# A fused decoder step on one core: the fourth group's output projection placed behind the second group's queries, with one planner table shifted by eight rows

## What is computed

```python
proj = hn @ w_in                      # hn = normed, modulated x
...                                   # retention and RG-LRU, gated and summed: merged
x = x + g1 * (merged @ w_out)         # the output projection
hn2 = rmsnorm(x, norm2_w) * (1.0 + sc2) + sh2
q = (hn2 @ w_q).reshape(T, 8, 256)    # 8 heads, two halves of 128
s1, s2 = q[..., :128] @ k1.T, q[..., 128:] @ k2.T       # 128 keys each
# top 16 of each, top 16 of their 256 sums: 8 * 16 = 128 experts a token
act = gelu(einsum('td,tkd->tk', hn2, u_tab[expert]))    # 128 rows of peer_u a token
x = x + g2 * einsum('tk,tkd->td', g * act, v_tab[expert])
y = rmsnorm(x, final_norm_w)
```

## Time and profile before

| | us |
|---|---|
| median of 3 runs | 3495.47 (3483.97 to 3502.88) |
| the profiled execution | 3501.91 |
| its span, first to last instruction | 3499.9 |
| TensorE busy | 3207.5 |
| VectorE busy | 2702.7 |
| GpSimd busy | 1826.4 |
| ScalarE busy | 1384.4 |

### The profile page before, as it was taken

One profiled execution on the slowest core, in us unless ns is written; L12 is line 12 of the kernel. 1 busy time (PEld: TensorE's weight loads), 2 busy tenths in 40 slices (PEclk: granted clock), 3 DMA queues, 4 the chain that ended last, 5 costly groups with the idle time before them and its releaser, 6 DMA issues.

```text
span 3499.9 us, 57521 instructions
## 1 busy us (share of the span) xinstructions
PE 3207.5 (92%) x18226; PEld 2582.7 (74%) x18226; DVE 2702.7 (77%) x5874; ACT 1384.4 (40%) x3092; POOL 1826.4 (52%) x1436
## 2 busy tenths in 40 slices
PE   6999998999999989887999999999998999998665
PEld 4777766666666668776878888888887888877555
DVE  3333357998998887889899999999998887667665
ACT  4444311333333221487555555555654565000110
POOL 0000002555567663345666766666665675766775
PEclk9999999999999999999999999999999999999888
DMA  8444454788899998789999999999999999999998
GB/s 269 150 150 150 140 173 150 258 273 283 264 336 331 317 331 305 270 281 361 380 392 391 403 389 393 388 391 397 398 356 374 388 406 407 396 410 407 372 353 301
DMA packets 429467, 1127.33 MB, mean 322 GB/s; under 512 B 42112, under 2 KB 166400, under 8 KB 429312
## 3 DMA queue, kind: packets, MB, share of 16 engines
q0 software_dynamic: 204800, 745.10, 57.0%
q1 hardware_dynamic: 219744, 370.53, 29.7%
q10 hardware_dynamic: 4768, 9.96, 0.8%
HBM read 1098.83 MB, written 26.62 MB: 322 GB/s over the span
## 4 chain that ended last, share of the span: by engine, by line
PE 38%; DVE 19%; DMA 13%; issue 12%; POOL 4%; ACT 1%; another core or an unknown queue 0%; POOLq 0%; DVEq 0%; ACTq 0%; SPq 0%
PE vacc L2355 21%; DVE rows L1754 8%; DMA rows<-in_peer_u,eidx 8%; PE scat L2289 5%; PE vacc L934 4%; POOL rows L1567 3%; DMA vbuf<-in_peer_v 2%; PE vacc L2269 2%; PE scat L2342 2%; PE vacc L905 1%; DVE oh1w L1835 1%; DVE hot L1650 1%; POOL W L1567 1%; DMA rows<-in_peer_v,eidx 1%; DMA rows<-in_peer_v,dots 1%
## 5 line engine op out<-in xcount | busy, mean ns | idle before, releaser
L1567 POOL DMA_INDIRECT rows<-in_peer_u,eidx x1080 | 1421.8, 1317 | 1456.3 <-DVE dots L1754 587.2
L2355 PE MATMUL vacc<-W,vbuf 128*128 (+1 forms) x6144 | 1426.7, 388 | 34.8 <-DMA vbuf<-in_peer_v 28.7
L1754 DVE CUSTOM_DVE_ANT_0 rows<-rows,htok 128x1024 f32<-128x1024 f32 x1080 | 1289.2, 1218 | 148.0 <-DMA rows<-in_peer_u,eidx 132.1
L2355 PEld LDWEIGHTS vacc<-W,vbuf 128*128 128x128 f32 x6144 | 1158.0, 193 | 185.6 <-issue 35.7
L2089 ACT ACTIVATE oh<-iota,e2s 128x128 bf16<-128x128 f32 x1536 | 486.4, 390 | 16.0 <-DMA scratch_sc<-sqb 7.0
L934 PE MATMUL vacc<-W 128*128 128x384 f32 x1280 | 431.6, 494 | 1.2 <-ACTq L811 1.2
L934 PEld LDWEIGHTS vacc<-W 128*128 128x128 f32 x1280 | 242.0, 192 | 169.1 <-issue 7.5
L2096 ACT ACTIVATE W<-scat 128x256 f32 (+1 forms) x320 | 122.9, 384 | 555.0 <-PE scat L2342 520.9
L2092 ACT ACTIVATE oh<-oh,ones 128x512 bf16<-128x512 bf16 x384 | 277.3, 722 | 12.5
L1835 DVE TENSOR_TENSOR oh1w<-oh,wpart 128x768 bf16<-128x768 bf16 x384 | 213.8, 557 | 62.6 <-PE scat L2342 43.1
L2289 PE MATMUL scat<-W 128*128 128x256 f32 (+1 forms) x1024 | 248.5, 398 | 5.4 <-DVE W L1636 5.4
(11 more groups left out here) (345 smaller groups left out, 3184.4 us busy)
## 6 DMA issues: line engine op xcount, KB each, us to landing
vbuf<-in_peer_v SPq DMA_DIRECT2D x384, 512.0 KB
W<-in_w_in SPq DMA_DIRECT2D x80, 512.0 KB
W<-in_wq SPq DMA_DIRECT2D x64, 512.0 KB
vbuf<-in_w_ada SPq DMA_DIRECT2D x9, 2048.0 KB, 8.0
rows<-in_peer_u,eidx POOLq DMA_INDIRECT x1080
W<-in_w_in SPq DMA_DIRECT2D x16, 1024.0 KB
W<-in_w_ada SPq DMA_DIRECT2D x3, 2048.0 KB, 15.8
W<-in_w_out SPq DMA_DIRECT2D x12, 512.0 KB, 10.0
```

Source lines behind the costliest of these rows:

```text
L1567: g.indirect_dma_start(row_of[s], None, table[:, :], bass.IndirectOffsetOnAxis(ap=picked, axis=0)).then_inc(landed[s], 16)
L1754: v.tensor_tensor_reduce(row_of[s], row_of[s], htok[:, home, :], 1.0, 0.0, ALU.mult, ALU.add, dots_of(t)[:, c:c + 1]).then_inc(used, 1)
L2355: mm = pe.matmul(vacc[:, k, :], vbuf[:, s, k * P:(k + 1) * P], W[:, e1, :].rearrange("p o t -> p (o t)"), start=(clear and s == 0 and k % ...
```

## The change

On TensorE `mixed(3)` moves behind `cross(1)`. `turn(0)` and `sum_squares(1)` move into `mixed(2)`, behind its chunks 1 and 3, and `turn(1)` behind it, ahead of `cross(1)`, with a wait until VectorE has finished `picks_high(1)`. On VectorE `residual(2)` takes `picks_high(0)`, `picks_low(1)` (behind chunk 1) and `scale(1)` (behind chunk 3) inside, `picks_high(1)` follows it, and `residual(3)` comes last, ahead of quarter -2, with ten jobs and eight pieces. Part B's last three `fill()` calls get no jobs. The table gives 341 jobs instead of 350 to part B's end, 400 instead of 388 to the start of quarter -2, and eight more at every cut from quarter 0 on. The projection's weight loads get two semaphores, so that its first part waits for the first two loads alone; the store of group 3's x goes behind eight more query weight loads on SyncE's queue; ScalarE's squares of group 3 go from inside `cross(1)` to behind it.

```diff
-AHEAD = 20
+AHEAD = 28
-HALF_B, END_B = 160, 350
+HALF_B, CALM_B, END_B, CALM = 160, 304, 341, 3
...
-            ("n", HALF_B, END_B, 12, 12, SLOTS * H // 2), ("z", END_B, q, 12, 12, 2 * KC),
-            ("r", q, q, 12, 14, 16), ("s", q, q + 4, 14, 15, 8)]
-    cuts = [q + 4, q + 36, q + 76] + [q + P + AHEAD + 64 * i for i in range(10)]
-    units = [15, 17, 19.5, 21.5, 23.5, 25.5, 27.625, 29.625, 31.75, 33.875, 36, 36, 36]
+            ("n", HALF_B, CALM_B, 12, 12, SLOTS * (H // 2 - 1)), ("o", CALM_B, END_B, 12, 12, SLOTS - CALM), ("z", END_B, q, 12, 12, KC + 4),
+            ("r", q, q, 12, 14, 16), ("s", q, q + 6, 14, 15, 8),
+            ("t", q + 6, q + 16, 15, 15.5, KC)]
+    cuts = [q + 16, q + 48, q + 84] + [q + P + AHEAD + 64 * i for i in range(10)]
+    units = [15.5, 17.5, 19.75, 21.75, 23.75, 25.75, 28, 29.75, 31.75, 33.875, 36, 36, 36]
...
             if k0 == 0:
-                pe.wait_ge(wo_in, 96 * g + 96)
+                pe.wait_ge(wo_low, 32 * g + 32)
...
+                pe.wait_ge(wo_in, 64 * g + 64)
...
-                slots = steps(plan[4])
-                residual(2, lambda: mixed_step(next(slots)))
-                picks_high(0)
-                scale(1)
-                residual(3, lambda: mixed_step(next(slots)))
+                slots = steps(plan[5])
+                residual(2, lambda: mixed_step(next(slots)), {1: first_turned, 3: lambda: scale(1)})
+                picks_high(1)
+                for at in slots:
+                    mixed_step(at)
...
+                slots = steps(plan[8])
+                residual(3, lambda: mixed_step(next(slots)))
+                for row in plan[9:]:
...
-                mixed(2)
-                turn(0)
-                sum_squares(1)
-                mixed(3)
-                cross(1, later)
+                mixed(2, {2: lambda: turn(0), KC // 2: lambda: sum_squares(1)})
+                turn(1)
+                pe.wait_ge(picks_ready, 2)
+                cross(1, later)
+                mixed(3)
                 cross(2, scattered)
```

More of the change, by code:

```diff
@@ L14 @@
+import itertools
 import math
@@ L1503, in _ @@
                 h_load(2)
-                for j in range(28, 64):
+                for j in range(28, 36):
+                    wq_load(j)
+                x2_store(3)
+                for j in range(36, 64):
                     wq_load(j)
@@ L1606, in _, with residual @@
                 v.sem_inc(sc_ps, 2)
-                def residual(g, between=None):
+                def residual(g, between=None, inside={}):
                     x = x2T[g]
@@ L1616, in residual @@
                             between()
+                        if m in inside:
+                            inside[m]()
                     if g == SG:
@@ L1915, in mixed_step, with first_turned @@
                         do_job(n)
+                def first_turned():
+                    picks_high(0)
+                    picks_low(1)
                 plan = stages()
@@ L1935, in _ @@
                     slots = steps(plan[2 + half])
+                    if half:
+                        slots = itertools.chain(slots, steps(plan[4]), [((), ())] * CALM)
                     for f in range(half * H // 2, (half + 1) * H // 2):
@@ L1944, in _ @@
                 picks_low(0)
-                slots = steps(plan[4])
-                residual(2, lambda: mixed_step(next(slots)))
-                picks_high(0)
-                scale(1)
-                residual(3, lambda: mixed_step(next(slots)))
-                summed_rows(SAMPLE)
[L1951 to L1954, removed]
-                        picks_high(1, nps)
-                scale(2)
+                slots = steps(plan[5])
[3 more added lines that the diff above has]
+                    mixed_step(at)
+                summed_rows(SAMPLE)
                 for at in steps(plan[6]):
                     mixed_step(at)
-                for row in plan[7:]:
+                scale(2)
+                for at in steps(plan[7]):
+                    mixed_step(at)
+                slots = steps(plan[8])
+                residual(3, lambda: mixed_step(next(slots)))
+                for row in plan[9:]:
                     i = row[0]
@@ L2261, in _, with mixed @@
                 mixed_high(pe, zA, 0)
-                def mixed(g):
+                def mixed(g, inside={}):
                     pe.wait_ge(mg_in[g % 2], 48 if g == 2 else 32)
+                    if g == NGRP - 1:
+                        pe.wait_ge(tr_free, turns(1, 1) + 1)
                     for m in range(KC):
+                        if m in inside:
+                            inside[m]()
                         pe.wait_ge(x2_ready, x2_begin(g - 1) + 2 * (m // 2) + 2)
@@ L2431, in later @@
                 def later(x):
[L2433 to L2436 removed]
+                    if x == 6:
                         sum_squares(2)
                 def scattered(x):
+                    if x == 0:
+                        pe.wait_ge(x2_ready, x2_end(3))
                     for b in (2 * x, 2 * x + 1):
```

30 lines of the change are left out of this document (13 added, 17 removed).

## The result

The changed kernel takes 3508.82 us (median of 22 runs, 3501.85 to 3517.3), the kernel before beside it 3496.67 us (22 runs). The ratio is 1.0027, 95% interval 1.0016 to 1.0039: 0.3% slower, 9 us by the ratio (the two medians are 12 us apart), inside the half per cent that the prediction called no change. The direction can be told all the same: run again beside later experiments it came to 1.0031 (1.0019 to 1.0043). The profiled execution spans 3507.3 us, 7.4 more than before.

A forecast was written before the change was run, and what follows sets the result against it. It took VectorE, TensorE and DMA as bounds by stage, gathers at the end. Terms +16.5 - 6.9 + 4.3 - 11.8 = +2.1 on the median 3495.5, rounded up to 3498 us; likeliest band 3488 to 3508, range 3480 to 3518.

The forecast's parts named there:

- the one from 3505 to 3513: Whole kernel: the two part-bounds, with quarter -2's delay of +16.5 us kept; chance 0.08.
- Part B's end: Last three fills without jobs: L1260 ends about 12 us earlier, no gap before L717, `mixed(2)` starts near 1307.4.
- From `mixed(2)` to the queries: TensorE idles 27 us for `picks_high(1)`, first query near 1366.5, slow clock costs `cross(1)` 3 us.
- Late rows: Inside `residual(2)`: waits for gathered rows among 28 jobs add 3 us, bounds 0 and 18.
- rival (a): Slower: rows come late in `residual(2)`, wait grows from 3 to 18 us, total 3513 or 3520; chance 0.17.
- rival (b): Slower: clock stays low, `cross(1)` at half clock takes up to 65 us more, total 3560; chance 0.03.
- Quarter -2: Its start, behind `mixed(3)` and `residual(3)`: about 1472 instead of 1455.5, +16.5 us.
- Quarters -2 and -1: VectorE taken as bound: four jobs fewer (-4.8) and pieces cut differently, together -6.9 us; V stream starts +9.6.
- the prediction's own sign: Wrong if quarters -2 and -1 are not shorter than 201 us, or the first V group doesn't take 562 or more.
- Its bound for the other case: V stream's start: if TensorE or ScalarE set the pace of quarters -2 and -1, the 6.9 us are lost: +16.5.
- The first V group: Start of the V stream: said to go at VectorE's pace, its pieces add +4.3 us, 0 if DMA alone sets it.
- The end: Row gathers behind the V stream: eight jobs fewer at 1.47 us each, -11.8 us.

The follow-up runs named there:

- back_between: Changed kernel with group 3's projection back in its old place ahead of the queries and the second turn in its middle; ratio to before 1.0011.
- order_alone: Changed kernel's moved order and part B's calm end, with the job and piece tables of the kernel before from quarter -2 on; ratio 1.0028.
- old_pieces: Changed kernel with the piece table of the kernel before; ratio to before 0.9990.
- calm_alone: Kernel before with only part B's calm end: its last three slots get no jobs; ratio 0.9983.
- changed_again: The changed kernel run once more as it is, against the kernel before; ratio 1.0031.
- lead_alone: Kernel before with a lead of 28 jobs, 12 instead of 4 in front of quarter -2, order and pieces as before; ratio 0.9989.
- back_pieces: As back_between, with the changed kernel's piece table, but 12 instead of 16 jobs ahead of quarter -2; ratio to before 0.9997.
- four_more: Changed kernel with four more jobs in quarter -1 and four fewer in quarter 0; ratio to before 1.0007.
- early_picks: Changed kernel with 16 instead of 28 jobs inside `residual(2)`, the other 27 behind `picks_high(1)`; ratio to before 1.0026.

## Why the prediction was right, and where its terms were off

The forecast, no change that can be measured, was right, and 3508.8 lies in its wider range, 3480 to 3518. It lies just above the band of 3488 to 3508 that had the largest chance, in the one from 3505 to 3513 that the prediction gave 0.08, for the case that the 6.9 us of quarters -2 and -1 are lost; they were. Its sum of +2.1 was too small: +7.4 in the spans, +9 by the ratio of 1.0027. Part of its nearness is luck: measured less forecast is -2.8 us at quarter -2, +9.0 in quarters -2 and -1, +3.5 in the first V group, +2.2 in the next two and -6.6 in the end, and these cancel to +5.3.

**Part B's end: right.** `mixed(2)` starts at 1305.57 (forecast 1307.4), with no gap ahead of L720, which takes 3.62 us (3.5). The prediction did not see that VectorE, rid of its jobs, would wait 8.7 us there for TensorE.

**From `mixed(2)` to the queries: right.** First query at 1363.60 (1366.5), 26.13 us of idle TensorE (27), 13.47 instead of 10.52 us for the first 48 matmuls, +3.0 (3); the granted clock was 0.54 in the first 7 us of them. The trace agrees so far with the Trainium skill, TensorE: Matmul & The Clock Gate, "HAM oscillation", in that the burst behind the gap starts slower; the price was 3 us and not more. Late rows cost about 0.5 us inside `residual(2)`, not 3, and most of the 5.4 us fell to the jobs behind it. So rival (a) did not come true, and rival (b) neither (0.98 from 1367 to 1436).

**Quarter -2: near.** 1469.2 instead of 1472; +13.7 for the forecast's +16.5, against an execution of the kernel before that came late to `mixed(2)` (29.4 us behind S). back_between shows that 5 to 7 us of it are the projection's new place. order_alone shows the mechanism: TensorE's idle time returns as waits in `residual(3)`.

**Quarters -2 and -1: wrong, the term that failed.** "VectorE is busy 182 of 201 us and I take it as the bound" gave -6.9; the measured stage is +2.1 (203.8 for 201.7), against the prediction's own sign that it must be shorter than 201. Its bound for the other case, V stream at +16.5, was the right one (+15.8). VectorE's share of 90% was read as a bound, but its idle time is a mutual wait with TensorE: four jobs cost 2 to 3 us, and the new piece table took 5.5 us more there in one pair and 2.4 in the other, where the prediction had -2.1 for it. Why a quarter of a unit less, cut elsewhere, lets the two engines wait longer for each other is not settled.

**The first V group: a wrong reading, half a right size.** The boundaries of the earlier trace rows at 2219 and 2717 are not those of the groups. At the starts of `finish()` the groups before take 530.8, 539.9 and 498 us, not 562, 498 and 509, and the first is no slower than the second. So the argument that the first group alone goes at VectorE's pace had no ground. The prediction's own sign, that it is wrong if the first group does not take 562 us, says so too. The group grew by 7.8 us (forecast 4.3). old_pieces, with the old pieces and still 537.3, rules the pieces out as the cause. The group's length goes with the lead: it takes 530.8 and 530.7 us in the kernel before and order_alone and 533.9 in calm_alone, all with the old lead, and 534.8 to 542.1 (changed_again) in the eleven with 28, of which lead_alone changes nothing else and takes 535.0. By marks, the time from the stream's start to its last matmul is 1569 to 1574 us in every kernel with 4 or 12 jobs ahead of quarter -2, and 1575 to 1582 in all with 16; this holds for both orders and both piece tables. What in the gathers' or the V blocks' timing makes it so was not tried.

**The end: right.** Forecast -11.8 for eight jobs. The rest was 273.8 and 271.6 us in the two kernels with the old lead, and 255.4 to 266.9, 261 in the mean, in the eleven with 28: about -11. The changed profile's own -18.4 is at the short end. Gathers still go at 1.45 us in the end (69 in this window; before 68):

```profile
3300.00:3400.00 100.00, 63.13 (x412) 58.87 (x410) 69.46 (x73) 10.21 (x26) 75.24 (x69) 0.85 1.00 381
```

**The sum by causes.** Picks and norm inside `residual(2)` gain about 6 us (170.9 to 164.6 at quarter -2), and the lead gives back in the end about what it costs. What the calm end gains is open, 0 to 12 us by its ratio. The projection's move loses 5 to 7 us, the piece table 7 to 8, and sixteen jobs ahead instead of twelve 4 us at quarter -2 and, with the same table, 9.5 at the stream's last matmul (back_between against back_pieces). The prediction had the parts that gain and the projection's move in one term, +16.5. It rightly took the half unit as covered by `residual(3)`'s waits in the changed kernel, as old_pieces shows; but the rest of the table stood in its sum at -2.1 + 4.3 = +2.2, and in the changed kernel it costs 8, most of it in quarters -2 and -1. In back_pieces, where VectorE waits for no chunk in `residual(3)`, the half unit costs its full 5.5 us ahead of quarter -2 and nothing comes back. So work should not go from a stretch where it is covered to one where it bounds.

## What to carry to other kernels

Where two engines take turns, move a step on one of them only after asking what its old place covered: the projection filled the wait for the picks, and behind the queries it left 26 us empty that came back as waits elsewhere. A busy share of 90% doesn't make an engine the bound; price a stage by both the full cost and zero, and add or remove a few units of its work to see which. Compare two executions of the same instructions before a difference of a few us is given a cause: here they lay 5 us apart counted from one mark and 0.1 from another. Cut a window at the program's own marks before arguing from its length, and separate a change of order from a change of tables: here parts that gain and parts that lose were hidden in a ratio of 1.0027, and without the projection's move, the new piece table and four of the jobs ahead it is 0.9968.

## What the runs showed that was not expected

The price of TensorE's slow start barely depends on the idle time ahead of it in these runs: 12.51 us for the same 48 matmuls behind a gap of 25.31 (four_more), 13.47 behind 26.13, 13.64 behind 26.45 (order_alone), 13.58 behind 8.78 (early_picks), and 10.52 with no gap. And the same program comes to the same point of part B up to 9 us apart in different executions, so that positions in two profiles are compared from a common mark and not from the span's start.
